# Feature-order matmuls stream their 256 tokens from last to first

## What is computed

```
x = x + fox_mixer(rms_norm(x, g), w_in, b_f, w_out)        # 1024 -> 3088, 1024 -> 1024
x = x + square(relu(rms_norm(x, g) @ w_up)) @ w_down       # 1024 -> 4096 -> 1024, twice
x = x + mla_mixer(...)
x = x + gla_mixer(...)                                     # 1024 -> 3088, 1024 -> 1024
x = x + (silu(conv(h @ w_a)) * conv(h @ w_u)) @ w_down     # 1024 -> 5632, 2816 -> 1024, twice
x = x + short_conv_mixer(...)                              # 1024 -> 3072, 1024 -> 1024
```

## Time and profile before

| | |
|---|---|
| Time, median of 3 runs | 1201.06 us (1200.96 to 1206.78) |
| Profiled execution, first to last instruction | 1203.7 us |
| TensorE matmuls busy | 1180.3 us (98%) in 9666 matmuls |
| VectorE busy | 875.4 us (73%) |
| ScalarE busy | 644.8 us (54%) |
| GpSimd busy | 295.9 us (25%) |
| HBM traffic | 168 GB/s over the span |

### The profile page before, as it was taken

The page is one execution under the profiler, slowest core; times in us unless marked ns, Lnnn a source line. Parts: engine busy times, 40 slices in busy tenths (PEclk is TensorE's granted clock), DMA queues, the critical chain, the costliest instruction groups (busy, mean ns, idle before and its releaser), DMA issues.

```text
span 1203.7 us, 26180 instructions
## 1 busy us (share of the span) xinstructions
PE 1180.3 (98%) x9666; PEld 1155.8 (96%) x9666; DVE 875.4 (73%) x1383; ACT 644.8 (54%) x1055; POOL 295.9 (25%) x285
## 2 busy tenths in 40 slices
PE   7999999999999999999999999999999999999997
PEld 6998999999997999999999999999999999999997
DVE  7776766656696766756667578888767678888853
ACT  4666555544446555543445456666544455665533
POOL 4001400012230500023400263344321025444421
PEclk9999999999999999999989999999999999999999
DMA  9643555555652655464544345554556555555461
GB/s 295 193 140 97 184 181 182 195 175 174 158 167 71 184 193 183 163 202 161 172 142 142 106 140 176 177 190 161 170 191 210 194 176 176 175 188 186 134 201 58
DMA packets 212097, 203.52 MB, mean 169 GB/s; under 512 B 11824, under 2 KB 211760, under 8 KB 212032
## 3 DMA queue, kind: packets, MB, share of 16 engines
q1 hardware_dynamic: 211888, 202.44, 52.6%
q10 hardware_dynamic: 144, 0.20, 0.1%
HBM read 201.57 MB, written 1.05 MB: 168 GB/s over the span
## 4 chain that ended last, share of the span: by engine, by line
PE 94%; DVE 3%; issue 1%; ACT 1%; POOL 1%; DMA 0%; DVEq 0%; POOLq 0%; ACTq 0%
PE gemm L719 28%; PE gemm L721 28%; PE gemm L720 28%; PE gemm L730 2%; PE gemm L731 1%; PE gemm L732 1%; DVE w_lo L1599 1%; PE score L910 1%; DVE act_a L1608 1%; PE score L1025 1%; PE misc L755 0%; DMA w_raw<-in_fox_w_in 0%; PE score L1028 0%; PE score L1128 0%; PE gemm L927 0%
## 5 line engine op out<-in xcount | busy, mean ns | idle before, releaser
L1599 DVE TENSOR_TENSOR w_lo<-w_raw,w_hi 128x1024 fp32r<-128x1024 f32 (+2 forms) x404 | 483.5, 1201 | 158.5 <-ACT w_hi L1238 157.1
L719 PE MATMUL gemm<-act_a,w_hi 128*128 128x256 f32 x1704 | 489.0, 287 | 9.3 <-DVE act_a L1608 8.8
L1238 ACT CAST w_hi<-w_raw 128x1024 fp32r<-128x1024 f32 (+2 forms) x404 | 401.3, 998 | 173.7 <-PE gemm L721 168.2
L720 PE MATMUL gemm<-act_a,w_hi 128*128 128x256 f32 x1704 | 484.6, 284 | 0.0
L721 PE MATMUL gemm<-act_a,w_lo 128*128 128x256 f32 x1704 | 484.4, 284 | 0.0
L719 PEld LDWEIGHTS gemm<-act_a,w_hi 128*128 128x128 f32 x1704 | 329.3, 193 | 14.0 <-DVE w_lo L1599 9.4
L720 PEld LDWEIGHTS gemm<-act_a,w_hi 128*128 128x128 f32 x1704 | 329.7, 193 | 0.1
L721 PEld LDWEIGHTS gemm<-act_a,w_lo 128*128 128x128 f32 x1704 | 329.5, 193 | 0.0
L719 PE MATMUL gemm<-hid,w_hi 128*128 128x256 f32 x864 | 242.1, 280 | 0.0
L720 PE MATMUL gemm<-hid,w_hi 128*128 128x256 f32 x864 | 241.7, 280 | 0.0
L721 PE MATMUL gemm<-hid,w_lo 128*128 128x256 f32 x864 | 241.7, 280 | 0.0
(11 more groups left out here) (268 smaller groups left out, 1406.7 us busy)
## 6 DMA issues: line engine op xcount, KB each, us to landing
w_raw<-in_ffn_w_up SPq DMA_DIRECT2D x76, 1024.0 KB, 5.2
w_raw<-in_ffn_w_down SPq DMA_DIRECT2D x32, 1024.0 KB, 4.9
w_raw<-in_gla_w_in SPq DMA_DIRECT2D x12, 1024.0 KB, 5.3
w_raw<-in_ffn_w_down SPq DMA_DIRECT2D x16, 768.0 KB, 4.1
w_raw<-in_sc_w_in SPq DMA_DIRECT2D x12, 1024.0 KB, 5.1
w_raw<-in_fox_w_in SPq DMA_DIRECT2D x11, 1024.0 KB, 5.8
w_raw<-in_ffn_w_down SPq DMA_DIRECT2D x16, 640.0 KB, 3.8
w_raw<-in_fox_w_out SPq DMA_DIRECT2D x4, 1024.0 KB, 4.9
```

What stands on the lines that cost most here:

```text
L719: nc.tensor.matmul(ps, wh[:, k, cols], act[:, k0 + k, 0, :], start=start and k == 0, stop=False)
L720: nc.tensor.matmul(ps, wh[:, k, cols], act[:, k0 + k, 1, :], start=False, stop=False)
L1238: nc.scalar.copy(split_half(w_hi, nc_, nj), raw_half(nc_, nj)).then_inc(w_hi_ready, 1)
L1599: nc.vector.tensor_tensor(split_half(w_lo, nc_, nj), raw_half(nc_, nj), split_half(w_hi, nc_, nj).bitcast(F32), ALU.subtract).then_inc(w_l ...
```

## The change

Inside `feature_block` the output view and the moving operand are both turned around along the token axis. Token 255 is streamed first and written to PSUM column 255 first; token 0 comes last. The stationary operand, the number and order of the instructions, the accumulation flags, the waits and signals and the place of each result are what they were. `token_block` and all other matmuls stay as they are.

```diff
-                last = None
+                to, last = ps[:, ::-1], None
                 for k in range(nk):
                     if tiles is not None:
 
                         pe.wait_ge(act_ready, tiles[k] if isinstance(tiles, list) else tiles + k + 1)
-                    nc.tensor.matmul(ps, wh[:, k, cols], act[:, k0 + k, 0, :], start=start and k == 0, stop=False)
-                    nc.tensor.matmul(ps, wh[:, k, cols], act[:, k0 + k, 1, :], start=False, stop=False)
-                    last = nc.tensor.matmul(ps, wl[:, k, cols], act[:, k0 + k, 0, :], start=False,
-                                            stop=stop and k == nk - 1)
+                    hi, lo = act[:, k0 + k, 0, ::-1], act[:, k0 + k, 1, ::-1]
+                    nc.tensor.matmul(to, wh[:, k, cols], hi, start=start and k == 0, stop=False)
+                    nc.tensor.matmul(to, wh[:, k, cols], lo, start=False, stop=False)
+                    last = nc.tensor.matmul(to, wl[:, k, cols], hi, start=False, stop=stop and k == nk - 1)
```

## The result

The changed kernel takes 1197.85 us (median of 13 runs, 1193.51 to 1198.5) against 1204.45 us of the kernel before beside it (13 runs, 1200.96 to 1206.78): a ratio of 0.9941, 95% interval 0.9929 to 0.9953. That is faster by 0.6%, small but clear of noise. A time is some 1.9 us longer than the span of the same execution (1193.54 against 1191.6 us in the profiled one).

The account below looks back on a forecast made before the run. TensorE's matmul count times start-to-start distance bounds the kernel: 8700 changed matmuls take 1036.5 of 1203.7 us. Terms (a) and (b) sum to 0 + 0, giving 1201 us; range 1130 to 1340 us for 8 in 10.

Parts of the forecast that it names:

- no effect: Likeliest case: the changed matmuls keep 120 and 117.3 ns, time 1195 to 1207 us; chance 0.32.
- (a): Moving operand read downwards in the changed matmuls: taken as zero, bounds 68 us saved to 137 us lost.
- fewer collisions: Rival: stream and weight load hinder each other less, act_a above all; 1188 to 1135 us, chance 0.30.
- more collisions: Rival: stream and weight load meet more often in the 8700 matmuls; 1272 or 1340 us, limit 120.7 ns, chance 0.18.
- (b): PSUM columns written downwards by the changed matmuls: taken as zero, upper bound 834 us lost.
- the pairs coming apart: Rival outside the range: read or write handles neighbouring columns singly, at half pace; 2038 us, chance 0.20.
- The stricter reading: PSUM write: downwards counts as not contiguous, which slows matmuls and speaks against the change by 834 us.
- The hindrance: Changed matmuls: moving stream and weight load hinder each other in SBUF by relative address; excess 8.7 ns on 5952, 6.0 on 2748.
- My distance without hindrance: Start-to-start distance of the changed matmuls with no hindrance, taken as 111.3 ns from plain float32 passes of 128 columns.
- The sign that I had named for it: Mean weight-load duration, 193 and 188 ns, should move with the distance if collisions are the cause, stay if PSUM is.

Follow-up runs that it names:

- the kernel at 448: Kernel before, ascending order, all four activation buffers moved to 448 bytes off the weights; 0.9665 of before without its two longest runs, median of all six 1166.18 us.
- the one at 96 and 0: Kernel before, ascending order, act_a and act_b moved to 96 bytes off the weights, hid and m_act level with them; 1.006 of before.
- Experiment 1: Changed kernel with PSUM written upwards again, so only the moving operand is read downwards; 0.9945 of before.
- experiment 2: Changed kernel with the moving operand read upwards again, so only PSUM is written downwards; 1.0009 of before.
- Experiments 3, 4 and 5: Kernels with buffers moved by pads, ascending like the kernel before, two of them descending like the changed one; from 0.9665 to 1.006 of before.
- the control: Kernel before, ascending order, every buffer, weights and activations, moved up by 32 bytes so that no relative address changes; 0.9996 of before.
- experiment 4: Act_a and act_b at 64 bytes off the weights, hid at 448: ascending like the kernel before 0.9811, descending like the changed one 1.0007 of before.

## Why the prediction held, and where it was off

**What held, and the luck in it.** 1197.85 us lies in the range, which from 1130 to 1340 us took in every case but one, and even in the 1195 to 1207 us of no effect. The ratio is the sharper test: 0.9941 is just beyond the 0.5% that I called no effect. The forecast's level was that of 3 runs, 1201.06 us, where the kernel before took 1204.45 us beside the changed one; the 3 us between forecast and result are thus less than the change itself, 6.6 us.

**The bound.** TensorE's start-to-start distance times the count was the right quantity. Adding up the change of distance over these matmuls, token-order ones included, in the traces gives 41.6 us less for the kernel at 448, whose span is 41.9 us shorter, and 6.2 us more for the one at 96 and 0, whose span is 6.6 us longer; in all twelve kernels of the experiments the two agree within 3.1 us, a size that the dips of the clock reach.

**(a) Read downwards.** I took zero, with the shift of phase as the size to expect: at most 16 us gained on act_a, 7 us lost on hid. The sign that I gave to each was right for both buffers and the size some six tenths and a sixth of it: 9.5 us gained, 1.1 us lost. The mechanism, a shift of how the two operands meet, was right and its size taken as zero where it was 0.7%, 8.4 us. The likeliest case, no effect, was thus not what came; the one that came is its neighbour, fewer collisions, at its weakest end: act_a's 118.4 ns lies between the 120 ns that I had put down for no effect and the 111 to 117 ns for fewer collisions. Experiment 1 shows that the read is the whole of it. The limit in the rival of more collisions was misread: 120.7 ns is act_a's distance plus 0.7; the mean of all 8700 before was 1036.5/8700 = 119.1 ns, so the limit was 119.8.

**(b) PSUM downwards.** Zero was right, as experiment 2 shows; with experiments 1 and 2 together the rival of the pairs coming apart falls, for read and write alike. The stricter reading of the Trainium skill's sentence on PSUM lines (Advanced Engine Details and Errata, PSUM Cachelines) is not borne out for the order alone: 256 neighbouring columns written downwards took the same 120 ns.

**The hindrance.** I inferred collisions of stream and weight load from 2.7 ns between two buffers. Experiments 3, 4 and 5 show that the relative address sets the distance, by up to 6.7 ns. That the partner is the stationary operand follows from the token-order matmuls, in which act_a and the weights change places and the offset is mirrored, together with the control; that it is the load of that operand beside the stream, and how the two get in each other's way (banks, lines, arbitration), is argued and was not measured. The sign that I had named for it, the duration of the weight loads, is a weak one: 193 and 190 ns stand beside the same 120 ns at 0 and 96 bytes. The sentence of the Trainium skill that I weighed (TensorE: Matmul & The Clock Gate, Part 2), that a weight load takes nothing from the running matmul, is not borne out here: the distance is anything from 113.3 to 120 ns by the offset between the two operands. My distance without hindrance, 111.3 ns, came near the best pattern seen, 113.3 ns, but in part by luck: it is the pace of plain float32 passes of 128 columns, which at 0.84 ns a column take 107.5 ns to stream, and no run shows a steady distance below 113.3 ns for 256 columns.

**More collisions.** The mean over all buffers did not get worse, but the rival was near: the same change at the offsets of experiment 4 is 2% slower than its ascending twin, and hid lost in the case itself.

**Clock.** That runs differ by their dips of the granted clock, some 4.5 us between 0.998 and 0.994, was not in my sum; it took a quarter of the effect out of the medians.

## What to carry to other kernels

When TensorE is bound by back-to-back matmuls with a weight load each, measure the start-to-start distance for each operand pair; if it differs between buffers of one shape, try the moving buffer's offset from the stationary one in steps of 32 bytes. Here pads of a few hundred bytes gave some 3%, the reversed order 0.6%. The best distance seen in descending order is 117.3 ns, in ascending order 112.9, by the counts; only six offsets were tried in descending order. Choose the offset by several executions, as the good ones have two patterns.

## What the runs showed that I had not expected

- The offset between moving and stationary operand moves the distance of 128x256 fp32r matmuls between 113.3 and 120 ns, and its effect goes on beyond 64 and beyond 128 bytes.
- The distance has a memory. At one address the engine runs a whole stage at 113.3 or at 117.8 ns, and a stall of 0.2 us in all at a stage's start switched it. The kernel at 448 spreads over 18 us from run to run; that this is the same switching in other executions is likely, but only one of them has a trace.
- The direction in which PSUM is written has no price: 1.0009 (0.9994 to 1.0023). For the moving operand's the sign depends on the offset, faster at 0 and slower at 64 and 448; whether it has a price of its own apart from that, no run tells.
- Act_a's offset also sets the pace of the matmuls in which it is the stationary operand, with the sign turned around.
